# Modulation rows on TensorE in the second attention's tail, index heads ahead of the gate, scale and shift inside the output projection

## What is computed

```
def ada_modulation(c, w, b):
    m = jax.nn.silu(c) @ w + b
    shift, scale, gate = jnp.split(m[:, None, :], 3, axis=-1)
    return shift, scale, 1.0 + gate
...
for layer in range(DEPTH):
    shift, scale, gate = ada_modulation(c, ada_w[layer, 0], ada_b[layer, 0])
    h = x * (1.0 + scale) + shift
    y = mixer_ab(h, ...) if layer % 2 == 0 else mixer_c(h, ...)
    x = layer_norm(DN_ALPHA * x + gate * y, ln_g[layer, 0], ln_b[layer, 0])
    shift, scale, gate = ada_modulation(c, ada_w[layer, 1], ada_b[layer, 1])
    h = x * (1.0 + scale) + shift
    y = squared_relu_mlp(h, mlp_w1[layer], mlp_w2[layer])
    x = layer_norm(DN_ALPHA * x + gate * y, ln_g[layer, 1], ln_b[layer, 1])
```

## Time and profile before

| | |
|---|---|
| three runs | 1522.02, 1516.97, 1521.10 us, median 1521.1 |
| profiled execution | 1516.26 us, its span 1514.3 us, mean PE clock 0.952 |
| busy | PE 1379.1 us (91%), PEld 1194.0 (79%), DVE 995.0 (66%), ACT 599.8 (40%) |
| MLP of layer 0 (205 to 387 us) | PE busy 181.0 of 182 us |
| transfers | 262.91 MB, mean 174 GB/s |

### The profile page before, as it was taken

One profiled execution on the slowest core, in us unless ns is written; L12 is line 12 of the kernel. 1 busy time (PEld: TensorE's weight loads), 2 busy tenths in 40 slices (PEclk: granted clock), 3 DMA queues, 4 the chain that ended last, 5 costly groups with the idle time before them and its releaser, 6 DMA issues.

```text
span 1514.3 us, 22680 instructions
## 1 busy us (share of the span) xinstructions
PE 1379.1 (91%) x8866; PEld 1194.0 (79%) x8866; DVE 995.0 (66%) x1437; ACT 599.8 (40%) x803; POOL 0.2 (0%) x4
## 2 busy tenths in 40 slices
PE   6977979999789789999869987999997899999997
PEld 1754679998788579999759986899987776899996
DVE  3666589778887567656766775755567545575554
ACT  2434343334345323433354322533345553443332
POOL 0000000000000000000000000000000000000000
PEclk8997989999999789999979998999998999999999
DMA  9744438787194235666425321454543310455540
GB/s 359 293 167 132 175 106 348 285 303 283 42 340 156 81 111 209 235 214 214 155 91 210 115 109 45 173 186 179 194 167 112 140 56 29 167 209 185 186 155 28
DMA packets 45842, 262.91 MB, mean 174 GB/s; under 512 B 5192, under 2 KB 6856, under 8 KB 21067
## 3 DMA queue, kind: packets, MB, share of 16 engines
q1 hardware_dynamic: 32672, 216.88, 39.5%
q10 hardware_dynamic: 13102, 45.09, 8.4%
HBM read 260.89 MB, written 1.05 MB: 173 GB/s over the span
## 4 chain that ended last, share of the span: by engine, by line
PE 76%; DVE 14%; ACT 4%; DMA 2%; issue 2%; SPq 0%; DVEq 0%; ACTq 0%
PE banks L523 22%; PE banks L524 21%; PE banks L525 21%; DMA A<-ada_w 2%; DVE w_lo L1564 2%; PE banks L730 2%; PE banks L1046 2%; PE banks L687 2%; ACT A L1101 2%; ACT w_hi L1085 1%; PE banks L633 1%; PE banks L669 1%; PE banks L828 1%; PE banks L700 1%; PE banks L915 1%
## 5 line engine op out<-in xcount | busy, mean ns | idle before, releaser
L1564 DVE TENSOR_TENSOR w_lo<-raw,w_hi 128x2048 fp32r<-128x2048 f32 x193 | 439.8, 2287 | 174.5 <-ACT w_hi L1085 171.3
L1085 ACT ACTIVATE w_hi<-raw 128x2048 fp32r<-128x2048 f32 x193 | 368.8, 1913 | 228.5 <-PE banks L525 218.2
L523 PE MATMUL banks<-hT_hi,w_hi 128*128 128x256 f32 x1432 | 412.1, 288 | 6.9 <-DVE hT_lo L1553 3.3
L524 PE MATMUL banks<-hT_lo,w_hi 128*128 128x256 f32 x1432 | 408.5, 285 | 0.0
L525 PE MATMUL banks<-hT_hi,w_lo 128*128 128x256 f32 x1432 | 408.3, 285 | 0.0
L523 PEld LDWEIGHTS banks<-hT_hi,w_hi 128*128 128x128 f32 x1432 | 278.0, 194 | 13.3 <-issue 7.1
L524 PEld LDWEIGHTS banks<-hT_lo,w_hi 128*128 128x128 f32 x1432 | 278.2, 194 | 3.1 <-issue 0.7
L525 PEld LDWEIGHTS banks<-hT_hi,w_lo 128*128 128x128 f32 x1432 | 278.0, 194 | 0.0
L523 PE MATMUL banks<-w_hi,R 128*128 128x512 f32 (+1 forms) x592 | 232.2, 392 | 4.1 <-DVE R L1553 2.1
L524 PE MATMUL banks<-w_lo,R 128*128 128x512 f32 (+1 forms) x592 | 230.3, 389 | 0.0
L525 PE MATMUL banks<-w_hi,R 128*128 128x512 f32 (+1 forms) x592 | 229.7, 388 | 0.0
(11 more groups left out here) (228 smaller groups left out, 1288.0 us busy)
## 6 DMA issues: line engine op xcount, KB each, us to landing
raw<-stream SPq DMA_DIRECT2D x193, 1024.0 KB, 4.9
A<-ada_w ACTq DMA_DIRECT2D x73, 512.0 KB, 5.5
A<-ada_w SPq DMA_DIRECT2D x16, 512.0 KB, 10.3
A<-ln_g ACTq DMA_DIRECT2D x4, 512.0 KB, 4.3
A<-ln_b ACTq DMA_DIRECT2D x4, 512.0 KB, 5.3
A<-ada_w SPq DMA_DIRECT2D x1, 1536.0 KB
A<-x_t SPq DMA_DIRECT2D x2, 512.0 KB, 13.2
X<-ada_w SPq DMA_DIRECT2D x1, 1024.0 KB
```

The lines of the kernel that those rows point to most:

```text
L523: pe.matmul(o, lh, rh, start=start, stop=False, skip_group_check=True)
L524: pe.matmul(o, lh, rl, start=False, stop=False, skip_group_check=True)
L1085: act.activation(w_hi[:, s, :], raw[:, s, :], ACT.Copy).then_inc(hi_done, 1)
L1564: v.tensor_tensor(w_lo[:, s, :], raw[:, s, :], w_hi[:, s, :], ALU.subtract).then_inc(lo_done, 1)
```

## The change

1. At the start, the 16 slices of shift and scale are loaded and used by k: both parts of slice k are awaited, then four quarters added.
2. The gate row is summed in bank 3 (no longer 5), two slices at a time on four quarters; the product that spreads it adds the quarters by a column pair `gate_sel`, made of the identity on DVE.
3. Index heads move forward: 0 to 2 ahead of the gate's spreading (their wait for the gate's read is dropped), 3 to 5 behind unit 5's rotation, 6 and 7 behind unit 6's, with one top-k round behind them. The second of the last rotations and one round stand in step 0 of the pipeline, the low part of unit 9 moves from ahead of it to step 4. The mask stays in step 3.
4. Sublayer 3 is computed as rows on PE: slices 0 and 1 are loaded early in the second attention, row steps 0 to 4 stand in its tail, 5 to 7 and the copy behind the first unit of the output projection. DVE's 16 sums and the clearing of its accumulator go.
5. For sublayers 1 and 3, columns (PE) and scale and shift (DVE) are made behind the second unit of the output projection, not in the join.

The core of the diff:

```diff
-        row_bank = {0: 4, "gate": 5, 1: 2}
+        mod_rows = {..., 3: arena(HTF + 1536, 512)}
+        row_bank = {0: 4, "gate": 3, 1: 2, 3: 2}
+        ROWS_OUT = {0: 1, "gate": 2, 1: 3, 3: 4}
...
-            s += rope(4) + [("gate_sum", 0, 5, 6, 0, 1)] + rest(AB + 5)
+            s += rope(4) + [("gate_sum", 0, 5, 6), ("gate_sum", 2, 0, 1)] + rest(AB + 5)
...
-            s += rope(14) + rest(AB + 7) + [f[3]] + rope(8) + [("gate0",)]
-            s += fills(AB + 5, "T", "h", "rope", [AB_TMP]) + rope(10)
-            s += [("index", h) for h in range(3)] + rest(AB + 8)
-            s += fills(AB + 6, "T", "h", "rope", [AB_TMP]) + rope(0)
-            s += [("index", h) for h in range(3, IDX_HEADS)] + rope(2) + rest(AB + 9)
+            s += rope(14) + rest(AB + 7) + [f[3]] + rope(8) + index(0, 3) + [("gate0",)]
+            s += fills(AB + 5, "T", "h", "rope", [AB_TMP]) + rope(10) + index(3, 6) + rest(AB + 8)
+            s += fills(AB + 6, "T", "h", "rope", [AB_TMP]) + rope(0) + index(6, IDX_HEADS) + [("topk",)]
             for i in range(8 + DUO_LAG):
                 s += [("duo", i, 0, 8)]
-                if i < TOPK // 16:
+                if i == 0:
+                    s += rope(2) + [("topk",)]
+                elif i < 4:
                     s += [("topk",)] * 2
...
-                if i == 6:
-                    s += rest(AB + 10)
+                if i in (4, 6):
+                    s += rest(AB + 9 + (i - 4) // 2)
             s += [("rows", 0, 0)]
-            return s + downs(AB + 7, [0, 1, 2, 3], {0: [("row_out", 1)]})
+            return s + downs(AB + 7, [0, 1, 2, 3], {0: [("row_out", 1)], 1: [("finish", 1)]})
...
-            s += score(5) + exps(5) + rope(7) + rest(CU + 15) + score(6) + exps(6) + spread(5) + score(7) + spread(6) + exps(7)
-            s += collect(5) + spread(7) + some(1) + collect(6) + some(1) + collect(7) + [("rows", 1, 0)]
-            return s + downs(CU + 12, [0, 1, 2, 3], {0: some(1), 1: some(len(parts))})
+            s += score(5) + exps(5) + rope(7) + rest(CU + 15) + score(6) + exps(6) + spread(5) + score(7) + row(0) + spread(6)
+            s += exps(7) + row(1) + collect(5) + row(2) + spread(7) + collect(6) + row(3) + collect(7) + row(4) + [("rows", 1, 0)]
+            return s + downs(CU + 12, [0, 1, 2, 3], {0: row(5) + row(6) + row(7) + [("row_out", 3)], 1: [("finish", 3)]})
...
-                part, k = i // KT, i % KT
+                part, k = i % 2, i // 2
...
+                        for k in range(KT):
+                            for part in range(2):
+                                pe.wait_ge(ld_start[(2 * k + part) % START_BUFS], 16 * (2 * k // START_BUFS + 1))
+                            for part in range(2):
+                                slice_rows(row_bank[0], 2 * part, k, START_BUF(A, 2 * k + part)).then_inc(ada_used, 1)
...
+                    for i, k in enumerate(ks):
+                        slice_rows(row_bank["gate"], 2 * i, k, gate_w[k], at == 0 and i == 1).then_inc(gate_used, 1)
...
+            def row_begin(s_):
+
+                act.dma_start(next_bias, ada_b[s_:s_ + 1, 0:2 * D]).then_inc(ld_bias, 16)
+                for k in range(2):
+                    load_row(s_, k)
...
                 elif kind == "ada_row":
-                    if a[0] + 2 < KT:
-                        load_row(a[0] + 2)
+                    if a[1] + 2 < KT:
+                        load_row(a[0], a[1] + 2)
...
+                        v.wait_ge(v_step, n["step"])
+                        spots = ident[:, :].rearrange("p (a b c) -> p a b c", a=2, b=2)
+                        v.tensor_tensor(gate_sel[:, :], spots[:, 0, :, 0], spots[:, 1, :, 0], ALU.add).then_inc(consts_ready, 1)
...
-                        if t == 1 and b in (0, 2):
-                            finish(b + 1)
```

More of the change, by code:

```diff
@@ L120, in two_block_kernel @@
         silu_c = sb("silu_c", [P, KT])
+        gate_sel = sb("gate_sel", [P, 2])
         zero8 = sb("zero8", [P, KT])
@@ L851, in gate @@
                     if first:
-                        r = slice(32 * h, 32 * h + 1)
-                        m = pe.matmul(B[6 + h][:, :], ones[r, :], mod_rows["gate"][r, :], start=True, stop=True)
+                        m = pe.matmul(B[6 + h][:, :], gate_sel[:, h:h + 1].to_broadcast([P, P]), mod_rows["gate"], start=True,
+                                      stop=True)
                         continue
@@ L1207, in mlp, with load_row @@
                 n["fill"] += PAIRS
-            def load_row(k):
+            def load_row(s_, k):
                 for part in range(2):
                     if k >= 2:
-                        act.wait_ge(ada_used, adas_before(1, k - 2, part + 1))
-                    act.dma_start(row_w[k % 2][part], ada_w[1, k, :, D * part:D * part + D]).then_inc(ld_rows[part][k % 2], 16)
+                        act.wait_ge(ada_used, adas_before(s_, k - 2, part + 1))
+                    act.dma_start(row_w[k % 2][part], ada_w[s_, k, :, D * part:D * part + D]).then_inc(ld_rows[part][k % 2], 16)
+            def row_begin(s_):
+                act.dma_start(next_bias, ada_b[s_:s_ + 1, 0:2 * D]).then_inc(ld_bias, 16)
+                for k in range(2):
+                    load_row(s_, k)
             def row_out(s_):
-                r = slice(0, 64 if s_ == "gate" else P)
-                act.activation(mod_rows[s_][r, :], B[row_bank[s_]][r, :], ACT.Copy).then_inc(row_ready, 1)
+                act.activation(mod_rows[s_], B[row_bank[s_]][:, :], ACT.Copy).then_inc(row_ready, 1)
             def gate_rows(b):
@@ L1268, in _ @@
                     if n["gates"] == 1:
-                        act.dma_start(next_bias, ada_b[1:2, 0:2 * D]).then_inc(ld_bias, 16)
-                        for k in range(2):
-                            load_row(k)
+                        row_begin(1)
+                elif kind == "row_begin":
+                    row_begin(a[0])
                 elif kind == "ada_row":
-                    if a[0] + 2 < KT:
-                        load_row(a[0] + 2)
+                    if a[1] + 2 < KT:
+                        load_row(a[0], a[1] + 2)
                 elif kind == "row_out":
-                    act.wait_ge(ada_used, adas_before(1, KT))
-                    row_out(1)
-                elif kind == "begin":
-                    ada_begin(a[0])
+                    act.wait_ge(ada_used, adas_before(a[0], KT))
+                    row_out(a[0])
                 elif kind == "fill":
@@ L1740, in _ @@
                 kind, a = step[0], step[1:]
-                if kind == "finish":
+                if kind == "finish" and a[0] != 2:
                     if a[0] == 0:
                         low(0, 0)
-                        finish(0)
+                    finish(a[0])
+                    if a[0] == 0:
                         for j in range(4):
```

73 lines of the change are left out of this document (29 added, 44 removed).

## The result

| | before | changed |
|---|---|---|
| median of 20 runs each | 1517.49 us (1510.08 to 1523.13) | 1523.18 us (1518.66 to 1527.50) |
| ratio | | 1.0038, 95% interval 1.0025 to 1.0051 |
| profiled execution | 1516.26 us, span 1514.3 | 1527.5 us, span 1525.5 |
| busy | PE 1379.1, DVE 995.0 us | PE 1379.3, DVE 974.0 us |

The change costs 0.38%, 5.7 us; the interval, 0.25 to 0.51%, reaches just under 0.3%, so the kernel is slower, and by about or over 0.3%. PE has the same work; DVE has 21 us less, and it did not help. The two profiled executions differ by 11.2 us, since that of the changed kernel lies 4.3 us above its median. What a part is worth is therefore taken from the experiments' ratios.

What follows compares the result with a forecast made beforehand. The chain of waits was three quarters TensorE: what counts is when PE gets its next work. -2.9 - 3.7 + 8.5 = +1.9 us on 1516.26 gives 1518.2; the runs' median 4.8 above gives 1523.0, range 1517.0 to 1529.5.

Steps and rivals of the forecast that it cites:

- the slow case: Whole kernel slower by over 0.3%: Rival 1, an unseen wait, or the forecast's upper end; chance 0.36.
- First attention: Start through the MLP's start: -2.8 at the first heads, -0.3 in the output projection, +0.2 at the start; -2.9 us.
- the start: Stretch to 60 us: bound by loads, so loading by k gains 0; DVE's extra copy and wait cost +0.2 us.
- The gate product: First attention, behind index heads 0 to 2: released at 85.1 instead of 83.19, a new wait of 1.9 us.
- Second attention, first half: DVE sums ahead of the rotations go: PE resumes 2.25 us earlier, no clock fall saves 1.4; together -3.7 us.
- Its tail: Second attention's tail and output projection: row steps on PE, wait for step 7's load, half clock, columns; +8.5 us.
- first unit of the projection ends: Second output projection: starts 1.3 us later but at full clock, so its first unit ends only 0.3 later.
- wait for step 7's slices: Second output projection: load issued at 541.2, second part landing 4.6 us later (bounds 3.6, 8.2); PE waits 3.5 us.
- half clock behind it: Second output projection, after the wait for step 7's load: half clock for 3.2 us, costing 1.6 us.
- Rival 1: Second attention's tail: clock does not return, projection starts at 540.2 instead of 534.65; +5.5, sum +7.4, 1528.5 us; chance 0.3.
- Rival 2: Idle time better filled: full clock at gate, tail, step 7 and layer 0's MLP; all four -4.8, 1516.3 us; chance 0.15.
- Rival 3: What the change moves is hidden on both sides, step 7's load landing within a step of issue; 1521.1 us; chance 0.05.

Runs made afterwards that it cites:

- e4: Changed kernel with the whole second attention's modulation (step list, DVE sums, columns, scale and shift) as in the kernel before: 1513.72 us, 0.9979 of the kernel before.
- e10: Changed kernel without the load of row step 7's slices in the second attention, so one of eight terms is not computed: 1516.13 us, 0.9995 of the kernel before.
- e1: Changed kernel with the start's loads and row products put back to the order by part: 1521.94 us, 1.0031 of the kernel before.
- e3: Changed kernel with the index heads back behind the fills of units 5 and 6: 1519.07 us, 1.0009 of the kernel before.
- e2: Changed kernel with the gate sum in two quarters and the gate product from one-row operands as before: 1522.13 us, 1.0030 of the kernel before.
- e12: Kernel before, with only two DVE sums moved from ahead of the second attention's rotations into its output projection: 1513.20 us, 0.9976 of the kernel before.
- e11: Changed kernel with index heads back and second attention as before, except two DVE sums moved from ahead of the rotations: 1507.97 us, 0.9939 of the kernel before.
- e5: Changed kernel with row step 7 and the row's copy moved behind the second unit of the second output projection: 1518.73 us, 1.0001 of the kernel before.
- e8: Changed kernel with index heads back behind the fills and row step 7 behind the second down unit: 1517.13 us, 0.9995 of the kernel before.
- e13: Changed kernel with the loads of the norm's weight and bias moved behind row step 7's load: 1522.82 us, 1.0030 of the kernel before.

## Why the prediction was right, and where it was not

**The number.** 1523.0 was said and 1523.18 came, but by two errors that cancel. The sum said +1.9 us; measured is +5.7. The three runs shown had their median at 1521.1, the twenty at 1517.49, so the base was 3.6 us too high. The case called likeliest, a change within 0.3%, was just missed; the outcome is the slow case, to which 0.36 was given.

**First attention: the size is met, the steps only in part.** -2.9 us was predicted, and e4, which has the change there alone, gives -3.2 (0.6 to 5.8 faster). The profiled execution shows less: MLP of layer 0 starts 0.6 us later than before, one of the prediction's own marks of being wrong, or 0.8 earlier with the unit's late landing of 1.4 taken off. The five executions with this first attention start it at 198.5, 198.5, 202.6, 202.6 and 202.8 us, the two with the old one at 202.2 and 203.9. So the gain of some 3 us is no steady shift: in these profiles it is there only where the clock returned early behind the first heads (e4 and e10, last section), which the prediction did not have. What it is made of stays open.

Of the steps, the start was right: bound by the loads (e1). *"The gate product is released at 85.1 instead of 83.19, unit 5's fill starts at 86.1 instead of 84.25"* failed in its second half. Release is at 86.77, which is 85.4 with the unit's late landing taken off. But I took the product at the old 1.06 us, and it needs 2.8: its selector has 128 rows where the old product had one, and the clock had fallen ahead of it. The steps compare 1.4 with 1.06 us at full clock (e3, before) and 2.8 with 2.0 at half (changed, e2). From the fill to the first heads the prediction has 29.1 us, and 29.1 was measured (89.57 to 118.70). So the missing 2.1 of the 2.8 us at the first heads is this product.

Two sums of the prediction are slightly off: four groups that go from 1.89 to 1.06 us save 3.3, not 3.4, and its terms up to the first heads add up to 115.0, not 115.2.

**Second attention, first half: right where it was worked out.** -3.7 was predicted, -3.6 stands in the trace from the later fills on, and e12 gives 3.6 us in the time. The mechanism, DVE's order of work ahead of the rotations, stands, with one correction: of the two sums named, at 441.12 and 446.45, e12 moved only the first (and the one before it), and that was enough. The half has two more terms in single executions that the sum lacks, falls of the clock: near 406 (1.9 us, in 9 of 14), and behind the shortened wait itself in e11. That *"after 1.65 us of idle its clock should not have fallen"* held in the changed kernel and e12 (1.71 us) and not in e11 (1.74 us).

**Its tail: right mechanism, sizes too small.** Predicted +8.5, in this trace +13.6. The other executions with the same tail put it at +10.4 (e1), +7.0 (e2) and +14.0 (e3), the mean of the four at +11.3:

| step | predicted | measured |
|---|---|---|
| first unit of the projection ends | +0.3 | +1.4 |
| steps 5 and 6 | 2.1 | 2.7, of it 0.60 for step 6's slices |
| wait for step 7's slices | 3.5 | 5.8 |
| step 7 | 1.05 | 1.9, at half clock |
| half clock behind it, second unit longer by | 1.6 | 1.7 |
| columns | 1.07 | 1.0 |
| from there to the MLP | -1.05 | -0.9 |

The term that failed most is *"its second part landing 4.6 us later"*: it landed 6.9 us later. The term is the median of the loads of the first attention. In the six executions in which the norm's two rows are issued ahead of it, as here, that second part took 6.9, 7.0, 7.0, 5.2, 4.5 and 4.5 us (changed, e3, e5, e1, e2, e8). The bound of 8.2 in the prediction covers them all; a single 4.6 does not stand for them, and why the landing is short or long stays open. Step 7 was charged at full clock although the sentence behind it let the clock fall: the two can't both be.

**Rival 1** said that the clock would not return in the tail. By its own mark, full by about 527, it was wrong: PEclk is 0.96 at 522. Of the rule in the Trainium skill's page "TensorE: Matmul & The Clock Gate", section "HAM oscillation — how this bites in real kernels", the trace agrees for the long wait only: steps behind waits of 0.20 and 1.57 us ran at full clock (1.06), the step behind 5.79 us at half (1.93). The page's own case has waits of some 3 to 5 us. In between, the steps behind 3.82 us (e13) and 4.34 us (e1) took 1.93 and 1.94 us, and the one behind 4.20 us (e2) 1.24.

**Rival 2** has none of its parts in the changed kernel's profile, but one of them in e2's: there the row products of the tail run at full clock from 518 (1.06 us), and the projection starts 28.0 us behind the last turn product, for 31.35 in the changed kernel. **Of the other marks**, the clock near 450 stayed full as said. PE resumed at 118.7 instead of about 115, the wait for step 7 was 5.8 instead of 3 to 4, and DVE did wait ahead of the scale and shift (14.27 us), because PE's columns came late.

**Rival 3**, a load of step 7 hidden between neighbours, was wrong as it stood, though e5 shows what would make it true: a unit of the projection in between.

## What to carry to other kernels

A load that can be issued only once its buffer is free needs its full landing time covered by work that stands ahead of the waiting step in PE's order, and that time is a range (3.6 to 7.0 us for the last load here), not one median. A step that waits there should move behind the next dense unit, as in e5. Before engine work is given to another engine, look for the few instructions of it that stand ahead of a waiting chain: moving 2 of 16 sums (e12) gave 3.6 us, as much as removing all 16 gave in the traces, without the price. An absolute time is no better than the base: predict the difference, and carry it over with care. And a stage of one profile is one draw: before a cause is read from two profiles, look at the same stage in every profile whose instructions are the same there, as with e13.

## What the runs showed of the hardware that I had not expected

**The clock's return is not fixed by the program.** The changed kernel, e4, e5, e10 and e13 have the same instructions up to the first projection, and it starts at 168.2, 164.0, 168.1, 164.0 and 168.1 us. Of e10, then of e5, order of time and stretches:

```profile
120.42 1.06 PE L816 MATMUL banks<-A,ones 1*32 1x512 f32 x8
...
120.00:121.00 1.00, 1.00 (x11) 0.34 (x9) 0.93 (x5) 0.48 (x2) 0.00 (x0) 0.78 0.00 0
```
```profile
121.98 1.93 PE L816 MATMUL banks<-A,ones 1*32 1x512 f32 x8
...
129.00:130.00 1.00, 1.00 (x9) 0.67 (x6) 0.90 (x6) 0.30 (x2) 0.00 (x0) 0.60 0.98 401
```

PE resumed at 116.93 and 118.48 us; full clock came 3.5 us later in the one and 11 us later in the other. That is worth 2.5 us or more at the projection, as much as many a step of the sum, and a profile is one draw of it: the 11.2 us between the two profiles shown against 5.7 between the medians is in part this.

**A landing is not fixed by the order of issue.** The Trainium skill's page "DMA: Bandwidth & Descriptors", section "Queues, rings and completion order", says that on each DMA engine a queue's descriptors are taken in ring order. By that, loads still in flight ahead on ACT's queue would hold the next one up, and in the changed kernel the second of the norm's rows landed only at 543.3 us, 2.9 us after step 7's first load was issued. But in e1 it landed 2.7 us after, and step 7's loads took 4.5 us there for 6.4 here. So no run here shows what queued loads add.
